# Row scales of the norms applied behind the matmuls: raw rows transposed half by half

## The reference

```
for l in range(2):
    h = rmsnorm(x, g_mix[l]);  parts = h @ w_in[l]          # 2760 columns
    q = rmsnorm(cq, g_q) @ w_uq;  kv = rmsnorm(ckv, g_kv) @ w_ukv
    o = [latent attention, top-64 sparse attention, retention * silu(rg)]
    x = x + o @ w_out[l]
    hf = rmsnorm(x, g_mlp[l]);  x = x + square(relu(hf @ w_ff1[l])) @ w_ff2[l]
x = rmsnorm(x, g_final)
h = rmsnorm(x, norm1_gain);  p = h @ w_in_2                 # RWKV, dilated attention and gate columns
x = x + (gated mix of both) @ w_out_2
h = rmsnorm(x, norm2_gain);  router -> top 2 of 32 experts; x = x + expert sum
```

## Time and profile before

| | before |
|---|---|
| median of 3 runs | 1681.44 us |
| profiled execution | 1682.91 us |
| its span, first to last instruction | 1681.1 us |
| mean granted TensorE clock | 0.966 of full |
| PE busy | 93% |
| DVE, ACT, POOL busy | 42%, 32%, 27% |
| read from HBM | 347.7 MB, 207 GB/s over the span |

### The profile page before, as it was taken

One profiled execution on the slowest core, in us unless ns is written; L12 is line 12 of the kernel. 1 busy time (PEld: TensorE's weight loads), 2 busy tenths in 40 slices (PEclk: granted clock), 3 DMA queues, 4 the chain that ended last, 5 costly groups with the idle time before them and its releaser, 6 DMA issues.

```text
span 1681.1 us, 22339 instructions
## 1 busy us (share of the span) xinstructions
PE 1564.4 (93%) x8602; PEld 1156.4 (69%) x8602; DVE 707.1 (42%) x1087; ACT 539.6 (32%) x820; POOL 450.2 (27%) x159
## 2 busy tenths in 40 slices
PE   7979899999979999998989989999799999999997
PEld 6767799998768799986866769975453434344343
DVE  2866365563875365553145735721321111211112
ACT  4546433334646443333435431101111111111010
POOL 3453334333462333434887311100000000000000
PEclk9989999999999999998989999979899999999999
DMA  5432245533432255545654500003499999999994
GB/s 189 163 119 76 101 137 190 200 131 141 163 119 76 101 176 184 182 174 163 202 200 142 214 24 32 1 1 123 180 421 428 428 428 428 429 429 428 428 429 187
DMA packets 44547, 351.79 MB, mean 209 GB/s; under 512 B 5059, under 2 KB 7023, under 8 KB 19887
## 3 DMA queue, kind: packets, MB, share of 16 engines
q1 hardware_dynamic: 43774, 349.35, 54.1%
q10 hardware_dynamic: 576, 1.12, 0.2%
q0 software_dynamic: 112, 0.17, 0.1%
HBM read 347.70 MB, written 1.07 MB: 207 GB/s over the span
## 4 chain that ended last, share of the span: by engine, by line
PE 61%; DMA 18%; DVE 9%; issue 5%; ACT 3%; DVEq 2%; POOL 1%; ACTq 0%; SPq 0%; POOLq 0%
DMA ring<-in_w_expert_up 17%; PE psum L984 12%; PE psum L986 12%; PE psum L985 12%; PE psum L1550 8%; PE psum L974 3%; PE psum L956 1%; PE psum L1576 1%; DVE arena L2025 1%; PE psum L1517 1%; PE psum L1050 1%; PE psum L1419 1%; DVE arena L2070 1%; PE psum L1069 1%; DVE h_split L1633 1%
## 5 line engine op out<-in xcount | busy, mean ns | idle before, releaser
L865 POOL TENSOR_TENSOR weights_split<-weights_raw,weights_split 128x2048 fp32r<-128x2048 f32 (+4 forms) x108 | 392.2, 3644 | 470.6 <-ACT weights_split L1645 470.4
L1645 ACT ACTIVATE weights_split<-weights_raw 128x2048 fp32r<-128x2048 f32 (+5 forms) x156 | 243.5, 1565 | 327.2 <-PE psum L986 326.8
L1550 PE MATMUL psum<-ring,arena 128*64 128x512 f32 x1024 | 225.5, 593 | 25.8 <-DMA ring<-in_w_expert_up 24.7
L1550 PEld LDWEIGHTS psum<-ring,arena 128*64 128x64 f32 x1024 | 73.4, 137 | 174.6 <-issue 174.6
L984 PE MATMUL psum<-weights_split,h_split 128*128 128x512 f32 (+3 forms) x464 | 181.0, 390 | 9.6 <-DVE arena L2287 6.8
L986 PE MATMUL psum<-weights_split,h_split 128*128 128x512 f32 (+3 forms) x464 | 178.0, 384 | 0.0
L985 PE MATMUL psum<-weights_split,h_split 128*128 128x512 f32 (+3 forms) x464 | 177.7, 383 | 0.0
L984 PE MATMUL psum<-h_split,weights_split 128*128 128x256 f32 x512 | 145.0, 283 | 0.8 <-DVE h_split L1633 0.8
L986 PE MATMUL psum<-h_split,weights_split 128*128 128x256 f32 x512 | 144.9, 283 | 0.0
L985 PE MATMUL psum<-h_split,weights_split 128*128 128x256 f32 x512 | 144.9, 283 | 0.0
L984 PE MATMUL psum<-weights_split,hidden_split 128*128 128x512 f32 (+1 forms) x320 | 125.9, 393 | 13.7 <-DVE hidden_split L1633 13.7
(11 more groups left out here) (354 smaller groups left out, 2157.3 us busy)
## 6 DMA issues: line engine op xcount, KB each, us to landing
weights_raw<-in_layer_w SPq DMA_DIRECT2D x94, 1024.0 KB, 4.8
ring<-in_w_expert_gate SPq DMA_DIRECT2D x32, 2048.0 KB, 16.1
ring<-in_w_expert_up SPq DMA_DIRECT2D x32, 2048.0 KB, 17.1
arena<-in_w_expert_down SPq DMA_DIRECT2D x32, 2048.0 KB, 13.4
weights_raw<-in_second_w SPq DMA_DIRECT2D x44, 512.0 KB, 4.3
weights_raw<-in_layer_w SPq DMA_DIRECT2D x6, 768.0 KB, 4.1
ring<-in_w_out SPq DMA_DIRECT2D x2, 2048.0 KB, 17.0
ring<-in_w_rwkv_out SPq DMA_DIRECT2D x1, 2048.0 KB, 9.7
```

The costliest lines, as they stand in the source:

```text
L865: eng.tensor_tensor(W.part(j, 1, n), W.raw(j, n), W.part(j, 0, n).bitcast(F32), ALU.subtract).then_inc(W.lo[W.pieces[j][1]], 1)
L1550: ins = pe.matmul(bank[half(j), :], xe[h][:, k, half(j)], w[j][:, k, :], start=(k == 0), stop=(k == KD - 1))
L1645: act.activation(W.part(j, 0, w), W.raw(j, w), ACT.Copy).then_inc(W.hi, 1)
```

## The change

- The transposes of "tr1" and "tr3", and those before the second block and the router, read raw x. They are done in two halves: banks 0 and 1 need only the first half of the columns (x_done counts T, or "wout" 0 and 1), banks 2 and 3 the rest. Around "tr3" and the router, PE runs "wout" 2 first, then the first transposes, then "wout" 3, and starts ff1 or the router on half of k.
- The reciprocal root is applied where projections leave PSUM: as a scale of ACT's copies of "proj", "rw", "qkv" and "gate", of DVE's copies in the second block, squared in the final adds of "ff2", and in the router's logits. Sums of squares follow the transposes on ACT instead of preceding them.
- At the second block the transposed raw x gets g_final times norm1_gain (a product made once), and its two roots are multiplied. The g_final norm of x itself stays. For the expert gather, ACT writes scaled rows to xn2.
- All filler matmuls at these places are gone; 12 matmuls run once at the program's start.
- Order: weight pieces 0 and 1 of the next stage are split before the transposed activations; block 1 of w_in is one piece (51 pieces in a layer instead of 52); `low_transposed` of "tr2" goes ahead of the second half of `select_keys(1)`, and the mask is signalled for each row tile; "mixT" is written to hTq; x is loaded first; the gains of a layer are loaded in the layer before; SP starts the second block's loads slot by slot; the memset of prev goes behind POOL's fourth piece.

```diff
+IN_PARTS = [1 if KD * w <= PIECE else 2 for _, w in IN_BLOCKS]
...
-    plan += mix[0:2] + interleave("wout", 2 * T, (4, 5, 2, 3), "V")
-    plan += interleave("tr3", 4, (0, 1, 2, 3), "V")
+    wout, turned_x = interleave("wout", 2 * T, (4, 5, 2, 3), "V"), interleave("tr3", 4, (0, 1, 6, 7), "V")
+    plan += mix[0:2] + wout[:3] + turned_x[:2] + wout[3:] + turned_x[2:]
...
-    split_by = dict(zip(range(12), "PPVVVVVVVPPP"))
-    p = [(("in", b, i), split_by[2 * b + i], ("proj", T * b + T - 1) if i else None) for b in range(len(IN_BLOCKS)) for i in range(2)]
+    p = [(("in", b, i), "V" if 1 <= b <= 3 or (b, i) == (4, 0) else "P", ("proj", T * b + T - 1) if i == IN_PARTS[b] - 1 else None)
+         for b in range(len(IN_BLOCKS)) for i in range(IN_PARTS[b])]
...
+            sp.dma_start(x, io["x"][0].rearrange("(t p) d -> p t d", p=P)).then_inc(x_loaded, 16)
             sp.dma_start(shared_c[:], io["shared_c"]).then_inc(consts_loaded, 16)
-            sp.dma_start(x, io["x"][0].rearrange("(t p) d -> p t d", p=P)).then_inc(x_loaded, 16)
+            sp.dma_start(gains2[:, 0:3 * KD], io["gains2"]).then_inc(gains2_loaded, 16)
...
-            for e in "PV":
-                sp.wait_ge(LW.lo[e], (DEPTH + 1) * len(LW.lo_order[e]))
             for j, (name, _, _) in enumerate(PW.pieces):
+                if j < RAWS2 and j % 2 == 0:
+                    LW.wait_lo(sp, LW.n - RAWS + j // 2, DEPTH - 1)
...
+            for _ in range(12):
+                pe.matmul(psum[:, 0, 0:SEQ], ident, causal, start=True, stop=True)
...
-                bridge(pe, units, ("tr1", 0), 18)
-                xn_ready.wait(pe, T, l)
-                transposes(pe, units, "tr1", xn)
-                bridge(pe, units, ("proj", 0), 9)
-                units.wait_emptied(*(("tr1", j) for j in range(4)))
-                for b in range(3):
-                    project_in(b, 0)
-                    project_in(b, 1)
+                x_done.wait(pe, T, l)
+                transposes(pe, units, "tr1", x, (0, 1))
+                x_done.wait(pe, 2 * T, l)
+                transposes(pe, units, "tr1", x, (2, 3))
+                units.wait_emptied(("tr1", 0), ("tr1", 1))
+                project_in(0, 0)
+                units.wait_emptied(("tr1", 2), ("tr1", 3))
+                project_in(0, 1)
+                project_in(1, 0)
+                project_in(2, 0)
+                project_in(2, 1)
...
+                mask_ready.wait(pe, 2, l)
...
+                project_out(1, 0, 0, range(4))
+                units.wait_emptied(("wout", 0), ("wout", 1))
+                transposes(pe, units, "tr3", x, (0, 1))
+                project_out(1, 0, 1, range(4), True)
...
+                units.wait_emptied(("tr3", 0), ("tr3", 1))
+                ff1_part(0, 0, 0, range(4))
+                units.wait_emptied(("wout", 2), ("wout", 3))
+                transposes(pe, units, "tr3", x, (2, 3))
+                ff1_part(0, 1, 0, range(4))
+                units.wait_emptied(("tr3", 2), ("tr3", 3))
+                for j in range(2):
+                    ff1_part(0, j, 0, range(4, KD))
+                    ff1_part(0, j, 1, range(KD))
...
+                        units.wait_emptied(("tr1", i))
...
-            bridge(pe, units, ("tr1", 0), 28)
-            pe.wait_ge(xn2_ready, T)
-            transposes(pe, units, "tr1", xn2)
-            units.wait_emptied(*(("tr1", j) for j in range(4)))
+            x_done.wait(pe, T, DEPTH)
+            transposes(pe, units, "tr1", x, (0, 1))
+            x_done.wait(pe, 2 * T, DEPTH)
+            transposes(pe, units, "tr1", x, (2, 3))
             project("rw", RW_BLOCKS)
...
+            project_out2(0, 0)
+            project_out2(0, 1)
+            project_out2(1, 0)
+            units.wait_emptied(("wout", 0), ("wout", 1))
+            transposes(pe, units, "tr2", x, (0, 1))
+            project_out2(1, 1)
...
+            route(range(4))
+            units.wait_emptied(("wout", 2), ("wout", 3))
+            transposes(pe, units, "tr2", x, (2, 3))
+            units.wait_emptied(("tr2", 2), ("tr2", 3))
+            route(range(4, KD))
...
-                x_done.wait(act, 1, l)
-                act.dma_start(gains[:], io["gains"][l]).then_inc(gains_loaded, 16)
-                sums_of_squares(act, [(x[:, t, :], xn[:, t, :], t, D) for t in range(T)], std_ready.sem)
-                split_high(SPLITS - 1)
+                    units.emptied_by(key, act.activation(dst, bank[:, 0:n], ACT.Copy, **scale), "A")
+                def split_after(*name):
+                    split_high(LW.index[name] + SPLITS)
+                split_high(1)
                 act.wait_ge(gains_loaded, l * 16 + 16)
                 high_transposed(act, units, "tr1", gain(G_MIX), hTp, hT_hi)
+                split_high(2)
+                x_done.wait(act, 2 * T, l)
+                sums_of_squares(act, [(x[:, t, :], xn[:, t, :], t, D) for t in range(T)], std_ready.sem)
...
-                        copy_out(("proj", T * b + t), proj[:, t, c:c + w], w)
+                        copy_out(("proj", T * b + t), proj[:, t, c:c + w], w, scale=rstd_x[:, t:t + 1])
...
+                split_after("out", 0, 0)
+                high_transposed(act, units, "tr3", gain(G_MLP), hTp, hT_hi, (0, 1))
+                split_after("out", 1, 0)
+                high_transposed(act, units, "tr3", gain(G_MLP), hTp, hT_hi, (2, 3))
+                units.wait_emptied(*(("tr3", j) for j in range(4)))
+                act.dma_start(gains[:], io["gains"][l + 1]).then_inc(gains_loaded, 16)
...
+            act.wait_ge(LW.used, (DEPTH + 1) * len(LW.used_order))
+            split_high(1)
+            act.wait_ge(gain_product, 1)
+            high_transposed(act, units, "tr1", gain2(2 * KD), hTp2, hT2_hi)
             act.dma_start(phase_c[:], io["second_c"]).then_inc(second_c_loaded, 16)
+            split_high(SPLITS2 - 1)
+            x_done.wait(act, 2 * T, DEPTH)
             sums_of_squares(act, x_rows(), std2_ready)
...
+            split_high(PW.index["rw", 0, 1] + SPLITS2)
             act.wait_ge(x_normed, 1)
             sums_of_squares(act, x_rows(), std2_ready)
-            act.wait_ge(gains2_loaded, 16)
-            high_transposed(act, units, "tr1", gain2(0), hTp2, hT2_hi)
+            split_high(PW.index["rw", 0, 2] + SPLITS2)
+            act.wait_ge(rstd2_ready, 1)
...
+            act_transposed(act, units, "tr2", gain2(KD), (0, 2))
             units.wait_emptied(("wout", 2 * T - 1))
             sums_of_squares(act, x_rows(), std2_ready)
-            act_transposed(act, units, "tr2", gain2(KD))
+            act.wait_ge(rstd2_ready, 2)
+            for t in range(T):
+                ins = act.activation(xn2[:, t, :], x[:, t, :], ACT.Copy, scale=rstd[:, t:t + 1])
+            ins.then_inc(xn2_ready, 1)
...
+                if j == 3:
+                    x_done.wait(pool, 2 * T, DEPTH)
+                    pool.memset(prev[0:1, 0, :], 0.0).then_inc(prev_zero, 1)
...
+            dve.tensor_tensor(gains2[:, 2 * KD:3 * KD], gains2[:, 2 * KD:3 * KD], gains2[:, 0:KD], ALU.mult).then_inc(gain_product, 1)
...
-                for b, i in ((1, 0), (1, 1), (2, 0), (2, 1)):
-                    split("in", b, i)
+                split("in", 1, 0)
+                std_ready.wait(dve, 1, l)
+                dve.reciprocal(rstd_x, std[:, 0:T]).then_inc(rstd_ready.sem, 1)
+                split("in", 2, 0)
+                split("in", 2, 1)
...
+                low_transposed(dve, units, "tr2", 1, gain(G_QKV), hTq, hT_hi, l)
                 select_keys(1, range(TOPK // 16, TOPK // 8)).then_inc(mask_ready.sem, 1)
-                low_transposed(dve, units, "tr2", 1, gain(G_QKV), hTq, hT_hi, l)
...
+                add_out(0)
+                add_out(1)
+                add_out(2)
+                low_transposed(dve, units, "tr3", 3, gain(G_MLP), hTp, hT_hi, l, (0, 1))
+                add_out(3)
                 split_low(LW, dve, LW.index["ff1", 0, 1], l)
-                norm(3)
-                low_transposed(dve, units, "tr3", 3, gain(G_MLP), hTp, hT_hi, l)
+                low_transposed(dve, units, "tr3", 3, gain(G_MLP), hTp, hT_hi, l, (2, 3), 2)
...
+                std_ready.wait(dve, 3, l)
+                dve.reciprocal(rstd_ff, std[:, 0:T])
+                dve.drain()
+                dve.tensor_tensor(rstd_ff, rstd_ff, rstd_ff, ALU.mult)
+                dve.drain()
                 for u in range(2 * T):
                     t, c = u % T, u // T
                     bank = units.wait_full(("ff2", u))
                     xc = x[:, t, c * 512:(c + 1) * 512]
-                    units.emptied_by(("ff2", u), dve.tensor_tensor(xc, bank, xc, ALU.add), "V")
-                dve.drain()
-                dve.sem_inc(x_done.sem, 1)
+                    units.emptied_by(("ff2", u), dve.scalar_tensor_tensor(xc, bank, rstd_ff[:, t:t + 1], xc, ALU.mult, ALU.add), "V")
+                    if t == T - 1:
+                        dve.drain()
```

(21 more changed lines are left out.)

222 lines of the change are left out of this document (108 added, 114 removed).

## The result

The changed kernel takes 1623.7 us (median of four executions, 1619.5 to 1624.8) against 1682.4 for the kernel before on the same chip: the ratio is 0.9647, with a 95% interval of 0.9625 to 0.9669. It is faster by 58.8 us. The forecast was 80.6 us less, 1600.8, with a range to 1619; the time lies 4.7 us above that range. The direction was right and the size was not, so the question of this part is where 22.9 us went. One execution of a later variant (SP's order changed) took 5585.8 us, over three times the others, and is left out of that variant's median.

A forecast was written before the change was run, and what follows sets the result against it. PE was taken to bound the feed-forward and DMA the expert stage, leaving gains at seams: 82.75 us summed, less 2.1 for handoffs, 80.6. From 1682.91 that gives 1602.3, less 1.5 over the median: 1600.8 us, range 1591 to 1619.

The forecast's parts named there:

- Start: Program start: with the norm gone, weights set the first product, at 20.2 instead of 25.8; gain 5.6 us.
- "tr3": Between the last "wout" product and ff1, in each layer: ff1 starts earlier despite one new wait; gain 11.2 us, twice.
- "tr2" of layer one: Before `project_q(0)` in layer one: low parts moved ahead of the key selection's second half; gain 10.1 us.
- router: Last add to router logits: logits at 1180.7 instead of 1185.05; gain 4.35 us.
- Seam between the layers: Last product of one layer to first of the next: first product at 390.9 instead of 403.25; gain 12.3 us.
- "tr2" in layer two: Same reorder in layer two: `project_q(0)` ends at 482.4 instead of 488.78; gain 6.3 us.
- Rival A: Attention part gives nothing back because DVE may pace it; the 16.4 of "tr2" go: 1617 us; chance 0.12.
- Second block: Seam into the second block: first product at 762.3, then PE loses 2.7 (0.8 to 4.5); gain 21.7 us.
- Rival B: Second block paced by ACT and POOL, DVE's g_final work colliding, pieces 6 and 7 late: 1608 us; chance 0.12.
- From there to the end: From SP's gate issue at 1212.02: 469 us untouched by the change, moved one for one by all that comes before.
- Rival C: PE falls to clock 0.50 at seven seams, losing 2.8 us each, 20 in all: 1620 us; chance 0.07.
- handoffs "that I can't see": Deduction from the summed gains for unseen handoffs: 0.3 us at each of seven seams, 2.1 in all.

## Why the prediction was right or wrong

**What bounds it.** Right. The expert stage kept its length to 2.3 us, ff1 moved as one piece, and every term lay at a seam.

**Start, "tr3", "tr2" of layer one, router.** Right, each within 1.3 us. The scales, put at nothing, cost little: DVE's add with a scale takes 0.75 for 0.69, ACT's copy 0.67 for 0.60. These are the steps in which I had followed each engine's list operation by operation, the new wait behind DVE's 2.28 among them.

**"Seam between the layers", 12.3.** The failed step is its sentence that the low parts come from DVE, "which is free after its last add", at 389.0. Free of work, but it had to jump. The jump takes 3.0 in the chain, the first product came 3.4 later than worked out (6.3 behind the last ff2 product instead of 2.9), and a low stretch of the clock followed. The pair of runs with the loop written out shows the cause (7.1 with the change, 0.7 without). The rows before couldn't have shown it: in the earlier trace rows DVE's low parts begin 12 us after the last product, behind idle time that hid the jump. That was the moment to give it a bound, and I gave it none.

**"tr2" in layer two, 6.3.** The mechanism was right and its size off. 5.4 stood at the end of `project_q(0)`. The step that failed is "What is late next is the mask ... only scores 2 and 3 need it": the mask is late for nobody, but DVE's operations that make it stand ahead of its ret products, and one took 2.39 beside POOL; and `project_q(1)` ran at the lower clock. Rival A, the attention part giving nothing back, is out: the reorder alone is worth 14 to 16.

**"Second block", 21.7.** The first product was right to 0.4 us. The step that failed is the loss behind it, 2.7 with bounds of 0.8 to 4.5, measured 6.2. I had priced DVE's two operations at the 6.74 of the earlier trace rows, where the two engines took turns. In the changed kernel they don't: the second operation stood behind all the pieces that POOL had ready, and the two took 8.27, 3.20 where POOL had only the end of a piece and its memset, 13.00 where it had four pieces. And I had left out SP's queue: I named g_final's DMA, not that the weights' pieces 6 on stand behind the nine that follow it. Rival B, with 8 to 10 us in this place, named the mechanism and was nearer in kind. The Trainium skill, page SBUF — State Buffer, section Terms, says that DVE and GpSimd lock a shared port pair for a whole instruction. The trace agrees that the two hold each other up, and the 6.74 fit one of POOL's instructions waited out by each of DVE's; 6.33 and 11.07 for one operation are two and four waited out, which that sentence of the page wouldn't give.

**"From there to the end ... this change doesn't touch, and all that comes before 1212 moves them one for one."** This failed by 7.1 us in the profile, 4.8 of it before 1212. For lora the runs show that the clock is the cause: the idle time is the same as before to 0.1 us, the low stretch lasts longer (products 11.1 for 8.2), and with fillers in the gap they take 6.4. The running sums took 5.35 for 3.65 at a low clock without a new wait in front of them; what put the low stretch there is open, since the fillers meant for it stand in no wait and take what they bring. The gather was no slower than before (5.62 for 6.32). Rival C had the price of this and a chance of 0.07. It had it at the seams. There the low clock was met only behind the two waits that were left, and it fell mostly in stages whose instructions hadn't changed at all. The Trainium skill, page TensorE: Matmul & The Clock Gate, section Why this matters for your kernels, says that idle gaps between bursts of matmuls bring the clock down; the gap of 3.49 at lora followed by 0.50 agrees, and I had weighed that rule only for the seams, not for the gaps that stayed.

**The last 2.3, in the experts.** The stage takes 464.2 to 465.1 in three profiles of the kernel before and its variants, and 465.8 to 466.9 in those of the changed kernel and its variants. With the clock held at 1.00 by fillers it still takes 466.0 to 466.3, and 465.8 in a version with five low stretches. That speaks against the clock but doesn't rule it out, since the fillers take PE's time. What adds 1 to 2 us stays open.

**The range.** It reached to 1619 for A and B, which both miss a piece. That DVE's jump, SP's queue and a low clock at lora all come at once wasn't a case. The handoffs "that I can't see", 2.1 for seven seams, were in truth one loop end of 3.0 and a conflict of DVE with POOL of several us.

## What to carry over

When a change takes away the filler work or an engine's idle time at a seam, list for each engine what it does in that time, control flow and queued small DMAs included, and price it by a run or as a bound: the end of a loop on the engine that now comes first cost 3 us here and nothing before. Where two engines hold each other up, as DVE and POOL did here, the price of an operation is a range: at the upper end it waits for all that the other has ready, and not only for one piece as in the rows of the kernel before. And stages that are only moved are not moved one for one as long as they have gaps of some us in front of matmuls. Look up each wait in the changed kernel's timeline before filling it: a filler where PE doesn't wait is work.

## What the runs showed of the hardware

- The end of DVE's loop over the layers took 3.0 us (362.58 to 365.6) in which the profile shows nothing; written out, DVE idled 0.80 in the same place.
- The same two DVE operations of 1024 elements from two SBUF tensors took 3.20 us beside the end of one of POOL's pieces and its memset, and 8.27 and 13.00 us where POOL had two and four pieces ready behind the memset; the second of them then took 6.33 and 11.07 and ended 1.1 us behind POOL's last piece. In the kernel before, with POOL's pieces back to back as well, they took 3.46 and 3.37, and POOL's pieces 3.33 instead of 2.4.
- A gap of 3.4 to 3.5 us ahead of the lora transposes came with the low clock in the profiles of the changed kernel and the kernel before, but not for equally long: in three windows of 4 us from 0.4 to 0.5 us ahead of the first transpose PEclk was 0.71, 0.50 and 0.51 in the changed kernel and 0.50, 0.69 and 1.00 in the kernel before, at nearly equal gaps and equal work. The lora products took 11.1 and 8.2 us.
- The running sums ran at a low clock in the changed kernel (5.35 us) and at 1.00 in the kernel before (3.65), with the same wait of 0.90 ahead of the matmuls before them.
- In the expert stage, bound by transfers, fillers that held the clock at 1.00 gained nothing clear: 466.0 us against 466.9 and 466.3 with five low stretches and no fillers.
